# A hybrid decoder layer in one kernel: constants in two parts, gates among the first groups, and VectorE splitting weights beside block 0's down projections

## What is computed

```
h = rmsnorm(x); z = h @ w_in
A = swish(group_layernorm(causal_dwconv31(z_value * sigmoid(z_gate))))
B = mlstm(q, k, v, i_gate, f_gate) with per-head layernorm, * sigmoid(o)
x = x + rmsnorm(concat(A, B) @ w_out)
up = causal_dwconv3(rmsnorm(x) @ w_up)
x = x + rmsnorm((gelu(up_a) * up_b) @ w_down)
x = x + (p @ w_ple) * sigmoid(rmsnorm(x) @ w_ple_gate)
```

## Time and profile before

| | |
|---|---|
| three timed runs | 2979.85, 2980.98, 3010.24 us, median 2980.98 |
| the profiled execution's own time | 2997.16 us |
| its span, first to last instruction | 2995.4 us |
| mean granted TensorE clock | 0.962 |
| busy: PE, DVE, ACT, POOL | 2755.9 (92%), 1723.9 (58%), 898.1 (30%), 310.0 us (10%) |
| moved by DMA | 660 MB, 220 GB/s |

### The profile page before, as it was taken

The page is one execution under the profiler, slowest core; times in us unless marked ns, Lnnn a source line. Parts: engine busy times, 40 slices in busy tenths (PEclk is TensorE's granted clock), DMA queues, the critical chain, the costliest instruction groups (busy, mean ns, idle before and its releaser), DMA issues.

```text
span 2995.4 us, 37504 instructions
## 1 busy us (share of the span) xinstructions
PE 2755.9 (92%) x14657; PEld 2646.5 (88%) x14657; DVE 1723.9 (58%) x3612; ACT 898.1 (30%) x1862; POOL 310.0 (10%) x112
## 2 busy tenths in 40 slices
PE   6688988989989999998999999999999987699996
PEld 6678877888889999997999999889999986699996
DVE  5965795987355655535556553555856534451533
ACT  3244432334333212423321223332112422221222
POOL 4521455533000000000000000000000000000000
PEclk9899998999999999999999999999999998799998
DMA  8646777886646666563666666356666552366666
GB/s 275 224 169 234 278 269 262 316 304 213 231 165 227 223 240 222 214 255 131 226 236 226 237 225 252 142 200 227 236 228 236 209 211 85 126 245 233 230 220 138
DMA packets 109035, 660.47 MB, mean 220 GB/s; under 512 B 20149, under 2 KB 20409, under 8 KB 39105
## 3 DMA queue, kind: packets, MB, share of 16 engines
q1 hardware_dynamic: 99424, 627.05, 58.5%
q10 hardware_dynamic: 9440, 31.07, 2.8%
HBM read 532.96 MB, written 125.11 MB: 220 GB/s over the span
## 4 chain that ended last, share of the span: by engine, by line
PE 75%; DVE 15%; ACT 4%; DMA 2%; issue 2%; POOL 1%; SPq 0%; POOLq 0%; ACTq 0%; DVEq 0%
PE proj L513 23%; PE proj L514 23%; PE proj L515 22%; DVE cv L1303 4%; DVE mix_room L1564 2%; DVE f_split L1591 2%; POOL w_split L491 1%; DVE mix_room L1561 1%; DMA w_raw<-in_w_units 1%; ACT w_split L791 1%; DVE temp_room L1395 1%; DVE mix_room L1210 1%; PE m L546 1%; PE m L664 1%; PE m L665 1%
## 5 line engine op out<-in xcount | busy, mean ns | idle before, releaser
L513 PE MATMUL proj<-h_split,w_split 128*128 128x416 f32 x2720 | 981.3, 361 | 34.2 <-ACT temp_room L1048 12.2
L514 PE MATMUL proj<-h_split,w_split 128*128 128x416 f32 x2720 | 958.9, 353 | 0.0
L515 PE MATMUL proj<-h_split,w_split 128*128 128x416 f32 x2720 | 953.0, 350 | 0.0
L513 PE MATMUL proj<-f_split,w_split 128*128 128x416 f32 x1600 | 586.3, 366 | 44.9 <-POOL w_split L491 20.5
L514 PE MATMUL proj<-f_split,w_split 128*128 128x416 f32 x1600 | 573.3, 358 | 0.0
L515 PE MATMUL proj<-f_split,w_split 128*128 128x416 f32 x1600 | 569.3, 356 | 0.0
L513 PEld LDWEIGHTS proj<-h_split,w_split 128*128 128x128 f32 x2720 | 515.0, 189 | 50.9 <-issue 23.5
L515 PEld LDWEIGHTS proj<-h_split,w_split 128*128 128x128 f32 x2720 | 515.8, 190 | 10.4
L514 PEld LDWEIGHTS proj<-h_split,w_split 128*128 128x128 f32 x2720 | 516.4, 190 | 2.5
L1303 DVE SCALAR_TENSOR_TENSOR cv<-a_ext,vecs,cv 128x416 f32<-128x416 f32 (+1 forms) x600 | 385.0, 694 | 0.0
L513 PEld LDWEIGHTS proj<-f_split,w_split 128*128 128x128 f32 x1600 | 309.9, 194 | 61.7 <-POOL w_split L491 21.8
(11 more groups left out here) (197 smaller groups left out, 2029.0 us busy)
## 6 DMA issues: line engine op xcount, KB each, us to landing
w_split<-w_kept SPq DMA_DIRECT2D x432, 1024.0 KB, 4.8
w_kept<-w_split SPq DMA_DIRECT2D x108, 1024.0 KB, 7.4
w_raw<-in_w_units SPq DMA_DIRECT2D x108, 512.0 KB, 5.3
x_resid<-in_x ACTq DMA_DIRECT2D x5, 1664.0 KB, 9.4
out_y<-x_resid ACTq DMA_DIRECT2D x10, 832.0 KB, 7.8
rows<-in_x ACTq DMA_DIRECT2D x4, 832.0 KB, 6.6
qkv<-in_x ACTq DMA_DIRECT2D x4, 832.0 KB, 4.5
qkv<-in_p ACTq DMA_DIRECT2D x5, 416.0 KB, 5.2
```

Source lines behind the costliest of these rows:

```text
L513: mm(dst, w_hi, a_hi, start=first, stop=False)
L514: mm(dst, w_hi, a_lo, start=False, stop=False)
L515: return mm(dst, w_lo, a_hi, start=False, stop=last)
```

## The change

**Constants in two parts.** SyncE issues x, `vecs` and `ident` (counted on `s_const`), the two first raw units, and then the other six constants (on `s_late`). `s_setup` has only the nine memsets, and the one of `a_ext` is cut to the 30 columns that need it. What is made of the late constants is counted on `s_ready`: ScalarE's high part of `wg` stands behind the first three weight units, VectorE's three instructions (`late_setup`) behind the first low parts of h. ScalarE waits for the second half of x only at its fifth square; high part 0 stands in front of the root, high parts 1 and 2 behind the high parts of h (before: 0 and 1 in front, 2 behind).

**Gates.** TensorE does them behind group 8 of the 12, ScalarE's `gate_rows` follows at the same place, and VectorE's `make_rows` stands behind tap 16 of the first pair.

**Splits on VectorE.** Nineteen low parts of block 0 (units u + 3 for the units u of the two down projections, where these are split at all: 11 and 8) go from GpSimd to VectorE. In the first half the 30 taps are cut in pieces, one per down group, and before each piece stand the low parts of the units that this group has set free. In the second half they stand in front of the group's addition. GpSimd's 89 others are written out instead of looped.

```diff
-            homes = {"vecs": vecs[:, :], "ident": ident[:, :], "sel": sel[:, :, :], "reset": reset[:, :, :],
-                     "mask": out_room[:, 0:2 * T], "w_gates": out_room[:, 2 * T:2 * T + KD * P],
-                     "b_gates": b_gates, "m_dec0": m_dec0}
+            homes = {"vecs": vecs[:, :], "ident": ident[:, :]}
+            late_homes = {"sel": sel[:, :, :], "reset": reset[:, :, :], "mask": out_room[:, 0:2 * T],
+                          "w_gates": out_room[:, 2 * T:2 * T + KD * P], "b_gates": b_gates, "m_dec0": m_dec0}
...
-            for r in range(SPLITS):
+            for r in range(RAW):
                 load_raw(r)
-                if r < RAW:
-                    continue
+            for name, home in late_homes.items():
+                sp.dma_start(home, t["consts"][name]).then_inc(s_late.sem, 16)
+            for r in range(RAW, SPLITS):
+                load_raw(r)
                 keep(r - RAW)
...
             for i in range(FRONT):
                 group(0, False, i, h, (lambda n: pe.wait_ge(s_h.sem, s_h.done(0, n + 1))) if i == 0 else None)
-            gates()
+                if i == EARLY - 1:
+                    pe.wait_ge(s_ready.sem, 3)
+                    gates()
...
-            for u in range(RAW):
+            high_part(0)
+            root(0, 0, m5, 1)
+            for i in range(KD):
+                high_h(0, 0, 0, i, h, x_next(i))
+            for u in range(1, RING):
                 high_part(u)
             for name, home in state_homes:
                 act.dma_start(home, t[name]).then_inc(s_states.sem, 16)
-            root(0, 0, m5, 1)
-            for i in range(KD):
-                high_h(0, 0, 0, i, h, x_next(i))
-            for u in range(RAW, RING):
-                high_part(u)
-            for i in range(FRONT):
+            act.wait_ge(s_late.sem, 16 * n_late)
+            fn(wg[:, 0, :, :], w_gates[:, :, 0:GATES], ACT.Copy).then_inc(s_gate_hi.sem, 1)
+            for i in range(EARLY):
                 front_group(0, 0, i, True)
             gate_rows(0, 0)
+            for i in range(EARLY, FRONT):
+                front_group(0, 0, i, True)
...
-                    conv(0, False, 0, marks, range(12, CW))
+                    conv(0, False, 0, marks, range(12, 16))
                     make_rows(False, 0)
+                    conv(0, False, 0, marks, range(16, CW))
                     conv(1, False, 0, [], range(CW // 2))
...
+                    dve.wait_ge(s_hi.sem, r + 1)
+                    v.tensor_tensor(w[:, slot, 1, :], w_raw[:, r % RAW, :], w[:, slot, 0, :].bitcast(F32),
+                                    ALU.subtract).then_inc(s_w[slot].sem, 16)
...
                     low_f(first + FH - 1)
+                    low_part((at.u_dnb if half else at.u_dna) + RING)
                     if half == 0:
-                        conv_next(0, range(FH, CW))
-                        conv_next(1, range(10))
+                        for i in range(KD):
+                            low_parts(at.g_dna + i)
+                            if i < 5:
+                                conv_next(0, range(FH + 4 * i, FH + 4 * i + 4))
+                            else:
+                                conv_next(1, range((10 * (i - 5)) // 3, (10 * (i - 4)) // 3))
                 for i in range(KD):
                     dve.wait_ge(s_evac.sem, s_evac.done(blk, at.g_dnb + i + 1))
+                    low_parts(at.g_dnb + i)
                     v.tensor_tensor(out[:, i, :], out[:, i, :], hf[:, i % 4, :], ALU.add).then_inc(s_dnadd.sem, 1)
```

More of the change, by code:

```diff
@@ L138 @@
 assert len(SPLIT_UNITS) == SPLITS
+SPLIT_ON_VECTOR = [SPLIT_NTH[u + RING] for first in (AT[False].u_dna, AT[False].u_dnb) for u in range(first, first + FH)
+                   if u + RING in SPLIT_NTH]
 def split_at(r):
@@ L492, in low_part @@
                                         ALU.subtract).then_inc(s_w[slot].sem, 16)
[L494 to L501 removed]
+            for r in range(SPLITS):
+                if r not in SPLIT_ON_VECTOR:
                     low_part(r, r)
@@ L1658, in _ @@
             program(NBLK - 1, True)
-SETUP = 12
+SETUP = 9
 STEPS_FIRST = 96
```

41 lines of the change are left out of this document (23 added, 18 removed).

## The result

The changed kernel took 2979.4 us (median of 20 executions, 2973.2 to 2986.9), the kernel before, on the same chip, 3000.0 us (20 executions, 2975.9 to 3015.3). The ratio is 0.994, 95% interval 0.9922 to 0.9957: it is faster by 0.6%, some 17 us by the means (the medians lie 20.6 us apart). The profiled execution took 2973.2 us (span 2971.3) beside 2997.2 (2995.4); it is the fastest of the changed kernel's twenty, so the two profiles lie further apart than the kernels do.

What follows compares the result with a forecast made beforehand. TensorE, busy for 92% of the span, was taken as the bound, with gains only where it idles or clocks lower. Terms 5.2 + 0 + 17.0 - 2.0 = 20.2 us off the 2981.0 median gave 2960.8 us, range 2948 to 2984.

Steps and rivals of the forecast that it cites:

- Rival A: First half's down projections: the 21 us hold isn't in the timed runs, so no gain, 2980.9 us; chance 0.20.
- term 1: Start: constants in two parts bring the first product earlier; 5.2 us gained (bounds 3 and 7.6).
- term 3: First half's down projections: VectorE's splits remove TensorE's wait on a held GpSimd split; 17.0 us gained (bounds 11 and 20.8).
- the two front terms: Front of block 0: constants in two parts, 5.2 us gained, and gates and rows moved earlier, 0 us gained.
- Term 2: Front: gates and rows earlier; the rows' 15.2 us wait goes, the one before `head_b(0)` grows to about 21; 0 us gained.
- The walk: Unit-by-unit estimate of when VectorE's splits are ready in the down projections: stalls of 2.1 us first half, 4.5 second.
- Term 4: Second half's down projections: VectorE's splits wait behind 10-step pieces; 2 us lost (bounds 6 lost, 3 gained).
- Rival B: Everything at the good bound, no addition held and VectorE's splits always in time: 31.4 us gained, 2949.6 us; chance 0.17.
- Rival C: Down projections: VectorE in program order paces the weights, 31 us lost instead of 6.6, together about 2990 us; chance 0.08.

Runs made afterwards that it cites:

- all_start_back: Changed kernel with VectorE making 75 of 108 low parts, late constants queued before the first raw weights, VectorE waiting for all eight constants at the start: ratio 0.9846.
- the version with VectorE's splits: Changed kernel with VectorE also making low parts in block 0's up projections and of units 7 to 18, 75 of 108: ratio 0.9828, 2951.5 us.
- front_only: Changed kernel with no split made by VectorE, so constants in two parts and the moved gates and rows alone: ratio 0.9995 against the kernel before.

## Why the prediction was right and wrong

**The step that failed most is the last one, the carrying over.** The sum against the profiled execution was 2977.0 us; the median is 2979.4, the profiled execution 2973.2. The prediction then took 16.2 us off, because the median of three executions of before was 2981.0, and so came to 2960.8, 18.6 us under the measured median. Two of these three were of a kind that 6 of the first 20 executions are and 3 of the 75 others; the median of the twenty is 3000.0, of all 95 3004.0. The profiled execution, 2.8 us from the first of these, was the better sample. Rival A read the gap of 16 us rightly as the question whether the hold is in the timed runs; seven of eight profiles have it (all eight are of executions of 2996 us and more). Its argument against itself, that waits which depend on chance would spread, was true, and the spread stood in the three numbers (2980, 2980, 3010); the text looked only at the two that agreed.

**The sum came near by luck.** It had 20.2 us for the 24.1 between the two profiles and for the 20.6 between the medians, but term 1 (5.2) wasn't there, term 3 gave 4.3 us more than forecast, and the second half's up projections gave 1.6 that no term had (109.7 us before, 108.1 now).

**The chances.** With the sum alone the gain is 20 us, 0.7%, inside "within 1%", which had 0.78. The outcome lies there too (0.6%). But the interval, 0.43 to 0.78%, excludes no change: with 20 executions on each side the comparison tells finer than the 1% that the prediction took for its limit, and a forecast of 20 us was a forecast of faster, not of the same. (The bounds of the four terms, added up, give 2949 to 2974, not the text's 2953 to 2973.)

**Term 1, 5.2 us gained, failed behind the start.** The start itself was right to 0.1 us (5.8 for 5.7, the additions took 6.02 us beside one split, as taken). "Only its earlier start counts" assumed that VectorE's work up to `head_a(0)` takes the same time. It took longer. From 44 us to `head_a(0)` GpSimd begins 13 splits in before, and two of them are held, for 10.4 and 10.1 us (and so cost VectorE nothing while they stand); the second still stands when `head_a(0)` begins, so 12 have been let in. 11 of VectorE's instructions take over 2 us there, 30.8 us in all. In the changed kernel's profile 14 splits begin, none is held, and 14 instructions take over 2 us, 38.7 us in all. At the same evacuation, 174 us in the profile of before, the eight profiles with the old front lie at -2.4 to +3.1 us (mean -0.2), the four with the whole new front and GpSimd's splits at -0.4 to +0.7 (mean +0.1): the two front terms brought nothing there. Once GpSimd's splits are out of VectorE's way, a start 4.9 us later makes `head_a(0)` 5.3 us later (all_start_back).

**Term 2, nothing gained, held:** the rows' wait went, `head_b(0)` has it (24.9 us for the 21 forecast, with `head_a(0)` 2.0 us later than before and not earlier). In the version with VectorE's splits the move, undone together with the places of six splits, is worth 6 us at `head_a(0)`, though not seen in the time, so "steps are moved, none removed" is true of the work and not of the waits.

**Term 3, 17.0 us gained, was mis-sized: 21.3.** The hold went as forecast, the split takes 1.22 us for 1.25. The walk's stalls, 2.1 us, and their lower clock, 1.7, didn't come: TensorE has no wait in the stretch, only the 4.1 us on the last gelu just ahead of it, which before has too, as it has the 4.1 us at clock 0.58 behind that. What rests on chance there is the 20.8: seven profiles of eight have the hold.

**Term 4, 2 us lost, was about right for the pair.** From the first of their products to the last the second half's down projections took 61.5 us before and 62.1 now, and to the next block's first product 65.0 and 66.5: 0.6 to 1.5 us lost. The stalls were 3.9 us for the walk's 4.5. What the term couldn't see is that the profile of before drew well here: GpSimd's splits cost TensorE 2.6 us in it but 8.0 in seven of ten profiles, in which the stretch takes 66.9 to 68.5 us instead of 61.5. Against those the change gains some 5 us.

**Rival B** (stalls nil, 20.8) was right of term 3 alone. **Rival C** didn't come: the raw weights' landings took 4.2 us at the median in the first down stretch (5.4 before), and no stall was seen in it.

## What to carry to other kernels

Before a gain is set against a median of a few runs, ask whether a wait in the profile is there in each: three times, two of them 30 us below the third, say that executions differ in kind, and their median says little. An engine that others hold up (here VectorE by GpSimd's splits) gives back an earlier start, because what happens beside it changes with the time at which it happens; look at the sum of its stretched instructions, not at its count of steps. And where two engines hold each other up, price the work on each by what it costs both: a split on GpSimd was 2.42 us beside and 2.15 us off VectorE, on VectorE it is 1.22.

## What the runs showed of the hardware

A GpSimd split issued while VectorE runs through instructions with two SBUF inputs, 0.50 to 0.56 us apart, has two fates. Mostly it is let in behind one of them and takes 2.4 to 2.9 us (five of 186 took 3.0 to 3.7), and the next step of VectorE takes 2.15 us more. Now and then it is held over a whole row of such instructions that follow without a gap: 10 to 11 us near 98 and 124 us in every profile with the gates and rows at their old place and GpSimd splitting in front, 17 to 21 us beside the 40 steps in seven of eight, 12 and 9 us beside 18 steps, 18 us beside 28 steps in front_only, 8 to 9 us through convolution steps, additions and low parts in the second half. Both fates were seen for the same instruction in the same run of steps. The Trainium skill, SBUF — State Buffer, "Who interferes with whom", has the first (the later one blocked for that instruction) and not the second. What chooses was not found, nor what the ends of the holds have in common; where in VectorE's 0.56 us period the split starts doesn't choose: held ones started 0.04 to 0.56 us after the step before, admitted ones 0.00 to 0.56.

What decides between 2 and 8 us of waits in the second half, and the stretch of 2360 to 2620 us that costs up to 7 us in some executions of either kernel, were not followed up.
